# Half-width local values products, an earlier first attention block and a new order

## What is computed

```
proj = jnp.einsum('bld,dc->blc', x, w_in)
...
dots = jnp.einsum('bqhd,bsd->bqhs', qi_blk, ki).astype(jnp.float32)
score = jnp.einsum('bqh,bqhs->bqs', w_blk.astype(jnp.float32) * idx_scale, jax.nn.relu(dots))
score = jnp.where(visible[None], score, -jnp.inf)
_, idx = lax.top_k(score, k_top)
...
p = jax.nn.softmax(jnp.concatenate([logits, sink], axis=-1), axis=-1)[..., :-1]
out = jnp.einsum('bckgqs,bcskd->bcqkgd', p.astype(v_band.dtype), v_band)    # group B
...
y = jnp.concatenate([ya * jax.nn.silu(ga), yb * jax.nn.silu(gb)], axis=-1)
x = layer_norm(ALPHA * x + y, ln_g, ln_b)
```

## Time and profile before

| | us |
|---|---|
| median of three runs (1453.73 to 1456.72) | 1456.59 |
| profiled execution, time | 1462.23 |
| its span, first to last instruction | 1460.4 |
| TensorE busy, whole span | 1359.3 (93%) |
| VectorE busy, whole span | 1130.6 (77%) |
| ScalarE busy, whole span | 896.8 (61%) |
| POOL busy, whole span | 629.6 (43%) |
| mean granted clock of TensorE | 0.964 |

### The profile page before, as it was taken

The page is one execution under the profiler, slowest core; times in us unless marked ns, Lnnn a source line. Parts: engine busy times, 40 slices in busy tenths (PEclk is TensorE's granted clock), DMA queues, the critical chain, the costliest instruction groups (busy, mean ns, idle before and its releaser), DMA issues. The chain is left out here.

```text
span 1460.4 us, 18810 instructions
## 1 busy us (share of the span) xinstructions
PE 1359.3 (93%) x6006; PEld 993.5 (68%) x6052; DVE 1130.6 (77%) x2215; ACT 896.8 (61%) x1687; POOL 629.6 (43%) x726
## 2 busy tenths in 40 slices
PE   7999999899999995798999799999999799999997
PEld 5888887698888874565655456655555565588886
DVE  3486879864899887778889999889898967257675
ACT  3395885873498736777775488885678676700010
POOL 2421332633422336466544256534336577423332
PEclk9999999999999996699999999999999899999999
DMA  7412232325232328233433132402011143134442
GB/s 241 127 60 80 87 105 80 117 91 154 73 109 94 101 90 174 66 89 87 113 92 88 45 83 56 104 21 64 27 28 26 39 133 118 44 122 146 144 148 83
DMA packets 106548, 136.85 MB, mean 94 GB/s; under 512 B 6643, under 2 KB 83383, under 8 KB 106191
## 3 DMA queue, kind: packets, MB, share of 16 engines
q1 hardware_dynamic: 93296, 93.23, 23.4%
q10 hardware_dynamic: 9504, 31.66, 5.5%
q0 software_dynamic: 3648, 10.76, 2.5%
HBM read 92.20 MB, written 42.34 MB: 92 GB/s over the span
## 5 line engine op out<-in xcount | busy, mean ns | idle before, releaser
L1644 DVE TENSOR_SCALAR_CACHE_REDUCE above<-dist,trial 128x512 bf16<-128x512 int32 (+13 forms) x224 | 345.9, 1544 | 28.9 <-POOL trial L1002 23.9
L1179 ACT ACTIVATE above<-dist,trial 128x384 bf16<-128x384 int32 (+13 forms) x224 | 280.8, 1254 | 60.8 <-DVE trial L1617 24.3
L1356 PE MATMUL psum<-x_hi,w_hi 128*128 128x512 f32 x640 | 251.8, 393 | 16.0 <-DVE x_lo L1693 10.6
L1356 PE MATMUL psum<-x_lo,w_hi 128*128 128x512 f32 x640 | 250.8, 392 | 0.0
L1356 PE MATMUL psum<-x_hi,w_lo 128*128 128x512 f32 x640 | 250.5, 391 | 0.0
L1290 ACT ACTIVATE prob<-psum 128x512 f32<-128x512 f32 x272 | 159.8, 593 | 115.8 <-PE psum L1506 54.6
L1748 DVE CUSTOM_DVE_ANT_0 junk<-psum,mask 128x512 bf16<-128x512 f32 (+3 forms) x320 | 184.4, 605 | 26.7 <-PE psum L1430 16.1
L1506 PE MATMUL psum<-prob,vw 128*65 128x512 f32 x376 | 184.8, 597 | 0.1
L1493 PE MATMUL psum<-qa_mix,ka_mix 128*128 128x512 f32 x272 | 162.4, 597 | 5.5 <-DMA qa_ext<-minus_max 3.7
L1430 PE MATMUL psum<-ka_ext,qa_ext 128*128 128x512 f32 (+3 forms) x320 | 134.1, 467 | 27.4 <-ACT ka_mix L1129 12.3
L941 POOL CAST w_hi<-raw 128x1024 fp32r<-128x1024 f32 x40 | 49.7, 1243 | 253.1 <-PE psum L1356 248.8
(11 more groups left out here) (161 smaller groups left out, 2906.8 us busy)
## 6 DMA issues: line engine op xcount, KB each, us to landing
raw<-w_tiles SPq DMA_DIRECT2D x40, 512.0 KB, 3.7
proj<-staged ACTq DMA_DIRECT2D x40, 512.0 KB, 3.3
qb_raw<-proj SPq DMA_DIRECT2D x32, 256.0 KB, 4.0
qa_raw<-proj SPq DMA_DIRECT2D x32, 256.0 KB, 4.5
yt_raw<-y_t SPq DMA_DIRECT2D x16, 512.0 KB, 5.1
x_row<-x_res SPq DMA_DIRECT2D x16, 512.0 KB, 3.9
out<-z ACTq DMA_DIRECT2D x16, 512.0 KB, 2.6
x_raw<-xT SPq DMA_DIRECT2D x12, 512.0 KB, 4.2
```

The costliest lines, as they stand in the source:

```text
L1179: nc.scalar.activation(above[:, 0, 0:n], src, ACT.Sign, scale=-1.0, bias=u, accum_out=count[:, 0:1]).then_inc(sign_counted, 1)
L1356: last = pe.matmul(psum[:, 2 * u + m, :], wt[:, u, k, :], xt[:, k, 512 * m:512 * m + 512], start=(k == 0 and q == 0), stop=(k == KT - 1 an ...
L1644: v.tensor_scalar(above[:, 1, 0:n], src, u, None, ALU.is_ge, ALU.add, accum_out=count[:, 1:2]).then_inc(own_counted, 1)
```

## The change

Three things, and what they need.

**Half columns.** `mix_b` takes only the 64 stationary columns of the key/value head g and writes them to rows 64g to 64g+63 of one bank. `gate_b` is then one multiply of all 128 rows.

**The first attention block prepared earlier.** The keys of group A are loaded into the memory of `values_hi` and `values_lo`, in two halves of 1024 keys, without a wait for the index sums; `split_values` waits until they are copied. `x_used` is now counted in both halves, and `last_tile(k)` names the moment when slice k of the last projection tile is done: loads of the first queries (k = 0) and of the bias (1), the constants of POOL (4) and the shifted values (5) wait for that alone. Buffers change places in memory accordingly (`qa_raw` comes first). VectorE's clearing goes to POOL (`fill`).

**The order.** Durations in the plan and in `AFTER` are changed, the norm products of the second half stand ahead of its last tile, and all numbers of `PREFER` are new.

```diff
-PREFER = {'above': -36689.1, 'band0': -163507.6, ...}
+FILLS = 7
+PREFER = {'above': -339679.4, 'band0': -2977.3, ...}
...
-    add("SP", 0.7, "load_keys_a", needs=[sums[-1], ("store", 1, 2)])
+    last = lambda k: ("product", 1, N_TILES - 1, k)
+    add("SP", 1.4, "load_keys_a", needs=[("store", 1, 2)])
...
-        add("PE", 1.8, "mix_b", b, needs=[("copy_b", b), ("shift_values",)], holds="banks2", until=("gate_b", b))
+        add("PE", 0.95, "mix_b", b, needs=[("copy_b", b), ("shift_values",)], holds="banks2", until=("gate_b", b))
...
-        keys_a_raw = flat(relu)
+        keys_a_raw = [values_hi[:, :, :].bitcast(F32).rearrange("p b n -> p (b n)")[:, 0:HALF],
+                      values_lo[:, :, :].bitcast(F32).rearrange("p b n -> p (b n)")]
+
+        def last_tile(k):
+
+            return (x_used, KT + k) if k < KT - 1 else (tile_mm, 2 * N_TILES)
...
             def load_keys_a():
                 sp.wait_ge(stored[0], 16 * (N_TILES // 2 + 2))
-                sp.wait_ge(summed, 4 * chunks_before(NPAIR - 2))
-                for r in range(2):
-                    sp.dma_start(keys_a_raw[HD * r:HD * r + HD, :], proj[ROW_KA:ROW_KA + HD, :]).then_inc(keys_in, 16)
+                for i in range(2):
+                    for r in range(2):
+                        sp.dma_start(keys_a_raw[i][HD * r:HD * r + HD, :],
+                                     proj[ROW_KA:ROW_KA + HD, HALF * i:HALF * i + HALF]).then_inc(keys_in, 16)
...
             def extra_rows():
-                pool.wait_ge(tile_mm, 2 * N_TILES)
+                pool.wait_ge(*last_tile(4))
...
+            def fill(top):
+
+                pieces = [(2, mask[:, 0, 0:P], 0.0), (2, mask[:, 1, 0:2 * P], 0.0), (2, mask[0:HD, 0, HD:P], -BIG),
+                          (2, mask[0:HD, 1, P + HD:2 * P], -BIG), (2, lb[:, :, 0:HD], 0.0), (5, vs[0:HD, 0, :], 0.0),
+                          (KT - 1, row_top[:, :], 0.0)]
...
-                        last = pe.matmul(psum[:, 2 + g, 2 * P * c:2 * P * c + 2 * P], keys, ptb[:, g, 2 * P * c:2 * P * c + 2 * P],
+                        rows = slice(HD * g, HD * g + HD)
+                        last = pe.matmul(psum[rows, 2, 2 * P * c:2 * P * c + 2 * P], keys[:, rows], ptb[:, g, 2 * P * c:2 * P * c + 2 * P],
                                          start=True, stop=True)
...
-                for g in range(2):
-                    rows = slice(HD * g, HD * g + HD)
-                    last = v.tensor_tensor(yt_b[rows, :, :].rearrange("p h (c q) -> p c h q", c=2),
-                                           psum[rows, 2 + g, :].rearrange("p (c h q) -> p c h q", c=2, h=4),
-                                           gate_b[rows, :, :].rearrange("p h (c q) -> p c h q", c=2), ALU.mult)
-                last.then_inc(b_gated, 1)
+                v.tensor_tensor(yt_b[:, :, :].rearrange("p h (c q) -> p c h q", c=2),
+                                psum[:, 2, :].rearrange("p (c h q) -> p c h q", c=2, h=4),
+                                gate_b[:, :, :].rearrange("p h (c q) -> p c h q", c=2), ALU.mult).then_inc(b_gated, 1)
```

149 lines of the change are left out of this document (72 added, 77 removed).

## The result

The changed kernel takes **1462.9 us** (median of 6 runs, 1460.4 to 1469.5) against 1455.4 for the kernel before (6 runs, 1453.7 to 1456.7). The ratio is 1.0058, 95% interval 1.0044 to 1.0072: slower by 0.6%, 7.5 us. I had forecast 1433 with a range of 1410 to 1455. The profiled execution took 1462.3 us, near its median, while that of before took 1462.2 and lies 7 us above its own; the two spans are therefore equal (1460.5 and 1460.4), and the loss shows in the medians alone.

What follows compares the result with a forecast made beforehand. Bounds: TensorE's row of work and, close by, VectorE's row up to the last mask. Terms -4.9 - 11 - 5 - 3 = -24 us took the median 1456.6 to 1433 us; range 1410 to 1455.

Steps and rivals of the forecast that it cites:

- The end of the projection, 540: Last projection product at about 540 us: 11.0 us of index products move behind it, 4.9 us of stall and half clock go.
- a projection that ends after 548: Sign in the profile after that would prove the prediction wrong; the last projection product was expected near 540.
- zero in itself: Moving 14 index pieces of pair 5, 11.0 us of TensorE, from before the last projection product to behind it costs nothing.
- I cost this at nothing: Keys' loads, copies and subtractions in the projection's second half lie under TensorE's products: 0, or some 7 us if cover fails.
- First scan: Behind the projection: first scan 10.4 us after the last product against 16.4, clock above 0.8; first logits about +33; -11 us.
- The next 65 us, -5: Stretch up to 650 us, losing 24 us at half clock: early searches stand later, -5 us, between 0 and -10.
- the gate, -3: Local values product on VectorE: one multiply replaces two, 11.0 us less work, credited -3 us, between 0 and -8.
- Local product, 0: Local values product on TensorE: 64 instead of 128 stationary columns change nothing; 0, possible gain up to 13.8 us.
- The rival of the halves side by side: Local values product's two halves overlap fully on TensorE, 13.8 us less: 1419 us; chance 0.26.
- a drain at either side of the product: Around the 16 local products: a tiling mode change drains TensorE, so the sum would only grow; not counted.
- The second limit: VectorE's row to the last mask: 546 us at 88% puts it at 1160, then 90 us of attention, ending at 1250.
- The searches fall behind: Rival: pair 5's search starts late, VectorE idles between steps; at 83% share 1469 us; chance 0.13.

Runs made afterwards that it cites:

- e14: e11 with the last 14 index pieces of pair 5, their relus and sums moved behind the last projection product, pair 5's conversion and first search steps behind them: 1471.1 us.
- e5: The changed kernel with the keys' load, ScalarE's copies and POOL's subtractions moved some 80 us later in their queues: 1455.5 us.
- e11: e9 with POOL's constants and clearing moved ahead of its subtraction for the index queries of pair 6: 1447.0 us.
- e1: The kernel before with only the half columns and the single gate added, every queue in its old order: 1450.5 us.
- e2: The kernel before with half columns, each head's half in a bank of its own, and its two gates of 64 rows kept: 1450.9 us.
- e3: The changed kernel with full columns and the two gates put back, its order kept: 1472.2 us.
- e7: e2 with both heads using stationary columns 0 to 63 and writing rows 0 to 63, the second head's local part left out: 1455.9 us, single run.
- e8: e1 with search steps of pairs 5, 6 and 7 counting only the first half of their keys on VectorE and ScalarE: 1441.6 us.
- e4: The changed kernel with the `PREFER` table, `AFTER` and plan durations of the kernel before: 1462.3 us.
- e6: e4 with the keys' load, copies and subtractions some 80 us later in their queues: 1462.1 us.
- e9: The changed kernel's buffers, waits, half columns and single gate, queues in the order before except pieces that must differ, keys early: 1450.9 us.

## Why the prediction was wrong, point by point

**The end of the projection, 540, was wrong in its price, not in its place.** e14 put it at 537.6 with the same 14 pieces. The changed kernel reached 553.4: the work left (10.5 us), the stall of the earlier trace rows went, and new waits came in, 8.6 us more than before in all. The keys' copies are 6.8 of these 13.4 us (e5, 546.6). The other 6.6 are waits that came with the new order and that no run took away; the longest in e5 are for POOL's `x_lo`, 3.26 us at 291.3 and 2.79 at 300.5, and for its index queries, 1.86 at 408.6. I had named a projection that ends after 548 as a sign of being wrong, and it was.
**Moved work is "zero in itself": this step failed.** It holds for TensorE's sum alone. The pieces come back in front of the first logits, with 2.9 us of VectorE for each two. I had let 21 us of work fill 33 us; the changed kernel took 38.5 us to the first logits, 5.5 more. e14, without the rest of the order, took 66.7, of which up to 15 are the place of the conversion.
**"I cost this at nothing" (keys early) was wrong.** I looked at evacuations behind the copies and not at the relus, which VectorE's sums and TensorE's next index pieces wait for. The price I had named for a failed cover, some 7 us, is what e5 gave back.
**First scan: right** (10.4 us behind the end of the last product forecast, 9.4 measured); the clock rose almost as far as forecast (0.78, not over 0.8). Its worth was not: e11 shows 3 to 4 us, where I had 11. What the transition gains in clock is gone again at the end: from the last product to the output product the clock is 0.94 in the changed kernel and in e1, which has the long gap, and behind the last mask it is 0.94 against 0.98.
**The next 65 us, -5, and the gate, -3: about zero.** e2 against e1 is the gate alone, 0.4 us. From first logits to output e3, the new order with full columns, takes 693.6 us, before 691.2 in an execution that lay 7 us above its median.
**Local product, 0: wrong by the whole term.** 8.5 us of TensorE's work in e1, 5 to 9 us of time. The rows of 64 columns between 65s that I had trusted write the same rows of PSUM as their neighbours, so they couldn't overlap; e7 is that case. The rival of the halves side by side was right in its mechanism, and too high in its price of 14 us. I had also set a drain at either side of the product aside by those rows; the steps into and out of it are in fact 0.1 us longer or more.
**The second limit fitted by chance.** 548.7 us of VectorE over 620.9 us are 88%, just as I had it, and with an end of 553.4 the sum gives the last mask at 1173 (measured 1174.5). But e8 breaks the rule. Behind the mask stood 101.5 us, not 90: only 8.6 us of TensorE's work had gone ahead of it (95.6 for 104.2), not 19.
**The searches fall behind** was the nearest rival: pair 5 begins 43 us later than before. Its masks still come on time (781.8, before 782.5), since the new order steps the search closer, and pair 6's come 7 us earlier than before (988.3, before 995.1). Only pair 7's, the last, come 8 us later (1174.5, before 1166.6), and what holds them up no run takes apart. In the old order with early keys (e4, e6) the rival's mechanism did show.

In sum: first logits forecast at 573 and found at 591.9, 19 us; 679 us from there to the output forecast and 684 found, 5 us. The forecast of 1433, these 24 us and 6 more give 1463: the profile of before stood 5.6 us above the median that I had, and that of after stands 0.6 below its own. The small 5 us is luck: my 679 counted the half columns at nothing, and without them the new order took 693.6 us (e3), 14.6 more. The columns, which I hadn't counted, hid 9.5 of these.

That the sum closes doesn't prove each term. e3 shows the columns and e5 the keys; for the moved pieces e14 shows the direction and not the price. What the rest of the new order costs behind the first logits stays open. The median of e5 stands 5 us above that of e1, though their profiled executions reach the output at the same time: e5's was 3.4 us faster than its median and e1's 1.8 slower, so the medians say which is faster, e1.

## What to carry to other kernels

Moving work behind a point to make that point earlier gained nothing here, where the work then stood in front of what the next stage waits for; ask where its followers (sums, copies) run, and which engine is free there. In a queue worked through in order, a step that is early for its user and waits for its own input holds up all behind it (here 5.6 us of waiting and 6.1 of copies, worth 7 us): put a copy that waits for a transfer behind the pieces on which another chain hangs. And take a new resource or buffer first with every other queue left as it was (e9, e11), since a table tuned to one plan says nothing about another.

## What the runs showed of the hardware

- Two float32 products of 64 stationary columns that write different halves of the PSUM rows run at the same time, also when another product stands between them in the program: 1.02 us for eight records, 1.87 us with the same columns.
- Going from products of 128 stationary columns to these of 64 and back has a price: 0.33 us from start to start ahead of them instead of 0.23, and 0.31 us from the last record to the next product instead of 0.22, or instead of 0.03 where a scan follows (e1 against before). In e7, where nothing overlaps, the steps are the same 0.33 and 0.31, and the product is slower than with 128 columns (1.87 for 1.73).
- A higher clock in the transition did not carry over: it is 0.78 there in the changed kernel and 0.55 in e1, yet 0.94 in both from the last product to the output product, and 0.94 against e1's 0.98 behind the last mask.
